# Joining the left-over rows of a feed-forward width of 2752, and the time-step columns of a state-space layer, into full tiles

## The reference

```python
D_FF = 2752                          # 21 * 128 + 64
def conv_ffn(h, w_up, conv_w, conv_b, w_down):
    u = h @ w_up                     # 1024 -> 2 * 2752
    up = jnp.pad(u, ((0, 0), (CONV_WIDTH - 1, 0), (0, 0)))
    c = conv_b + conv_w[0] * up[:, 0:S]
    for tap in range(1, CONV_WIDTH): # CONV_WIDTH = 3
        c = c + conv_w[tap] * up[:, tap:tap + S]
    gate, val = jnp.split(c, 2, axis=-1)
    return (jax.nn.silu(gate) * val) @ w_down
...
# first layer of the second block: of h @ w_in_a, 16 columns are the time steps of 16 heads
dt = jax.nn.softplus(dt_raw.astype(f32) + dt_bias.astype(f32))
```

## Time and profile before

| | |
|---|---|
| time, median of 3 runs | 1671.64 us (1670.78 to 1671.84) |
| span of the profiled execution, first to last instruction | 1668.0 us |
| PE busy | 96% of the span, 8762 matmuls |
| PEld, DVE, ACT, POOL busy | 81%, 62%, 50%, 6% |
| DMA, mean over the span | 81 GB/s |
| mean granted clock of TensorE | 0.986 |

### The profile page before, as it was taken

One profiled execution on the slowest core, in us unless ns is written; L12 is line 12 of the kernel. 1 busy time (PEld: TensorE's weight loads), 2 busy tenths in 40 slices (PEclk: granted clock), 3 DMA queues, 4 the chain that ended last, 5 costly groups with the idle time before them and its releaser, 6 DMA issues.

```text
span 1668.0 us, 23619 instructions
## 1 busy us (share of the span) xinstructions
PE 1597.5 (96%) x8762; PEld 1357.1 (81%) x8762; DVE 1027.0 (62%) x1784; ACT 833.5 (50%) x1598; POOL 94.2 (6%) x159
## 2 busy tenths in 40 slices
PE   7998899999999999999999999999999998999988
PEld 6987787887788888887788889788877787888877
DVE  5567986886555656555234434797666556548873
ACT  6645566665434555553123213786453563336763
POOL 1321400001000000000000000000000000000000
PEclk9999999999999999999999999999999999999999
DMA  7531012122543333332222232111122212131011
GB/s 214 149 92 43 31 58 70 45 70 83 169 136 83 92 94 86 96 88 93 93 90 81 92 101 87 47 51 53 53 76 85 68 51 76 59 112 54 26 51 51
DMA packets 148960, 135.61 MB, mean 81 GB/s; under 512 B 9072, under 2 KB 142960, under 8 KB 148864
## 3 DMA queue, kind: packets, MB, share of 16 engines
q1 hardware_dynamic: 143744, 120.04, 23.6%
q0 software_dynamic: 4544, 13.67, 2.5%
q10 hardware_dynamic: 576, 0.60, 0.1%
HBM read 124.07 MB, written 7.34 MB: 79 GB/s over the span
## 4 chain that ended last, share of the span: by engine, by line
PE 76%; DVE 13%; ACT 6%; issue 4%; DMA 1%; POOL 0%; DVEq 0%; SPq 0%; ACTq 0%
PE bank L299 21%; PE bank L301 20%; PE bank L300 20%; PE bank L1239 2%; PE bank L1253 1%; PE bank L1216 1%; ACT whi L277 1%; DVE wlo L284 1%; DVE pr L1404 1%; DVE ptl L1409 1%; PE bank L2783 1%; PE bank L2083 1%; ACT pr L3200 1%; DVE nm L1392 1%; ACT pr L1297 1%
## 5 line engine op out<-in xcount | busy, mean ns | idle before, releaser
L299 PE MATMUL bank<-hh,whi 128*128 128x512 f32 (+3 forms) x1208 | 466.1, 386 | 17.3 <-DVE wlo L284 6.3
L301 PE MATMUL bank<-hh,wlo 128*128 128x512 f32 (+3 forms) x1208 | 455.7, 377 | 0.0
L300 PE MATMUL bank<-hl,whi 128*128 128x512 f32 (+3 forms) x1208 | 455.0, 377 | 0.0
L277 ACT ACTIVATE whi<-wraw 128x2048 fp32r<-128x2048 f32 x111 | 212.6, 1915 | 285.4 <-PE bank L301 285.3
L284 DVE TENSOR_TENSOR wlo<-wraw,whi 128x2048 fp32r<-128x2048 f32 x101 | 231.3, 2290 | 157.0 <-ACT whi L277 156.2
L299 PEld LDWEIGHTS bank<-hh,whi 128*128 128x128 f32 (+2 forms) x1208 | 229.9, 190 | 60.7 <-issue 6.0
L301 PEld LDWEIGHTS bank<-hh,wlo 128*128 128x128 f32 (+2 forms) x1208 | 229.6, 190 | 43.5
L300 PEld LDWEIGHTS bank<-hl,whi 128*128 128x128 f32 (+2 forms) x1208 | 230.4, 191 | 38.8 <-issue 0.2
L299 PE MATMUL bank<-ah,whi 128*128 128x512 f32 (+1 forms) x240 | 87.6, 365 | 3.9 <-DVE al L3323 2.5
L1409 DVE TENSOR_TENSOR ptl<-bank,pth 128x128 fp32r<-128x128 f32 (+3 forms) x128 | 56.7, 485 | 52.4 <-ACT pth L1315 52.0
L1297 ACT ACTIVATE pr<-bank,nm 128x128 f32<-128x128 f32 (+3 forms) x128 | 66.8, 533 | 42.5 <-DVE nm L1392 42.5
(11 more groups left out here) (417 smaller groups left out, 3081.7 us busy)
## 6 DMA issues: line engine op xcount, KB each, us to landing
wraw<-in_w_in_a_dram SPq DMA_DIRECT2D x52, 512.0 KB, 4.5
wraw<-in_w_up_dram SPq DMA_DIRECT2D x42, 512.0 KB, 4.8
wraw<-in_w_in_dram SPq DMA_DIRECT2D x34, 512.0 KB, 4.8
wraw<-in_w_in_c_dram SPq DMA_DIRECT2D x18, 512.0 KB, 4.8
wraw<-in_w_down_dram SPq DMA_DIRECT2D x16, 512.0 KB, 4.0
wraw<-in_w_out_a_dram SPq DMA_DIRECT2D x16, 512.0 KB, 4.0
aside<-stage POOLq DMA_DIRECT2D x20, 256.0 KB, 2.3
wraw<-in_w_attn_br_dram SPq DMA_DIRECT2D x8, 512.0 KB, 4.3
```

The lines of the kernel that those rows point to most:

```text
L277: act.activation(whi[:, p], wraw[:, p], ACT.Copy).then_inc(w_hi_done, 1)
L299: pe.matmul(out, ws[0], hs[0], start=first, stop=False)
L300: pe.matmul(out, ws[0], hs[1], start=False, stop=False)
L301: return pe.matmul(out, ws[1], hs[0], start=False, stop=last)
```

## The change

1. **Up.** The last up item is loaded with its 64 value columns right behind its 64 gate columns, and is one tile of 24 matmuls on 128 columns: gate in rows 0 to 63 of the bank, value in rows 64 to 127. The parameters of the value columns are put on rows 64 to 127 too. ACT and DVE treat the two row halves by as many instructions as before, 64 rows each; the Silu reads rows 0 to 63 and writes rows 64 to 127. The high part of the 64 products goes to rows 64 to 127 of the last slot of `yh`, the low part to rows 0 to 63 of the same slot (`low_beside`).
2. **Down.** The last 64 rows of `w_down` are loaded twice, to rows 0 to 63 and 64 to 127 (a DMA of 128 rows of 1 KB, before 64). Two matmuls on 128 rows (`beside`: high and low part of the weight by that slot of `yh`) stand where three on 64 rows stood.
3. **Time steps.** DVE writes the low part of the 16 columns into `whi` itself, 32 columns behind the high part, and no longer makes the whole `wlo` of that item. The tile is 16 matmuls on 48 columns into bank 4, and DVE adds the two row groups: `daf` takes two chained operations, before one. The wait for `drained` ahead of this tile is gone, and the next stage waits for `drained` to be two less, so no longer for the time-step tile.

```diff
         def pairs(b, c0, cols):
             s = wraw[:, b % 2]
-            return [(s[:, :, 0:cols], v[:, :, bass.ds(c0, cols)]), (s[:, :, P:P + cols], v[:, :, bass.ds(c0 + DFF, cols)])]
+            return [(s[:, :, 0:cols], v[:, :, bass.ds(c0, cols)]),
+                    (s[:, :, cols:2 * cols], v[:, :, bass.ds(c0 + DFF, cols)])]
...
+        def low_beside(dve):
+            dve.wait_ge(f_high, FT + 1)
+            dve.tensor_tensor(yh[GATE, FT, :], fa[VALUE, LJ, :], yh[VALUE, FT, :].bitcast(F32),
+                              ALU.subtract).then_inc(f_low, 1)
...
+        LAST, LJ = n0 + FT, FT % 2
+        GATE, VALUE = slice(0, FREST), slice(P - FREST, P)
         @block.tensor
         def _(pe):
             halved_items(pe, n0, ready, between)
-            each(1, pe, lambda b, j, i, f, n: products(pe, b, j, i, f, n))
+            each(1, pe, lambda b, j, i, f: products(pe, b, j, i, f))
+            item_ready(pe, LAST)
+            pe.wait_ge(drained, m0 - 4 + 2 * FT + 1)
+            tile_of(pe, LAST, 0, bank[2 * LJ][:, :], H).then_inc(tiles, 2)
...
+            straight(act, LAST, LJ, 0, FT)
+            split_hi(act, LAST + 2)
+            gate(act, LJ, FT, GATE, VALUE)
+            high(act, LJ, FT, VALUE)
...
+            conv(dve, LAST, LJ, 0, FT)
+            product(dve, LJ, FT, VALUE)
+            split_lo(dve, LAST + 2)
+            low_beside(dve)
...
                             pr_ = [(s[:, 0:FT - 16, :], v[:, 16:FT, cols]),
-                                   (s[0:FREST, FT - 16, :], mat[FT * P:DFF, cols])]
+                                   (s[:, FT - 16, :], mat[FT * P:DFF, cols].unsqueeze(0).to_broadcast([2, FREST, IC]))]
...
+            def beside(pe, p, t, out, ts):
+                cs = slice(P * t, P * t + P)
+                pe.matmul(out[:, ts], whi[:, p, FT - 16, cs], yh[:, FT, ts], start=False, stop=False)
+                return pe.matmul(out[:, ts], wlo[:, p, FT - 16, cs], yh[:, FT, ts], start=False, stop=True)
...
-                        k, cs = FT - 16, slice(P * t, P * t + P)
-                        mm = passes(pe, out, (whi[0:FREST, p, k, cs], wlo[0:FREST, p, k, cs]),
-                                    (yh[0:FREST, FT, :], yl[0:FREST, FT, :]), False, True)
+                        mm = beside(pe, p, t, out, slice(0, S))
...
             item_ready(pe, n0 + 6)
-            pe.wait_ge(drained, m0 + 9)
-            tile_of(pe, n0 + 6, 0, bank[0][0:SSD_H, :], H, cols=SSD_H).then_inc(tiles, 2)
+            for k in range(KT):
+                for part in H:
+                    mm = pe.matmul(bank[4][0:LO + SSD_H, :], whi[:, (n0 + 6) % 2, k, 0:LO + SSD_H], part[:, k, :],
+                                   start=(k == 0 and part is hh), stop=(k == KT - 1 and part is hl))
+            mm.then_inc(tiles, 2)
...
-            split_lo(dve, n0 + 6)
+            dve.wait_ge(w_hi_done, n0 + 7)
+            dt = (n0 + 6) % 2
+            dve.tensor_tensor(whi[:, dt, :, LO:LO + SSD_H], wraw[:, dt, :, 0:SSD_H],
+                              whi[:, dt, :, 0:SSD_H].bitcast(F32), ALU.subtract).then_inc(w_lo_done, 1)
...
-            dve.tensor_scalar(daf[0:SSD_H, :], bank[0][0:SSD_H, :], pcol("dt_bias", rows=SSD_H), None,
-                              ALU.add).then_inc(drained, 1)
+            dch(dve, dve.tensor_scalar(daf[0:SSD_H, :], bank[4][0:SSD_H, :], pcol("dt_bias", rows=SSD_H), None,
+                                       ALU.add))
+            dve.tensor_tensor(daf[0:SSD_H, :], bank[4][LO:LO + SSD_H, :], daf[0:SSD_H, :], ALU.add).then_inc(drained, 1)
...
-            pe.wait_ge(drained, m0)
+            pe.wait_ge(drained, m0 - 2)
             tile(0)
```

More of the change, by code:

```diff
@@ L89, in tiles, with value_tiles @@
         return out.reshape(n, P).T
+    def value_tiles(v):
+        out = tiles(v)
+        out[P - FREST:, FT] = out[:FREST, FT].copy()
+        return out
     def rows(v):
@@ L107, in pack_params @@
         "convw_g": np.concatenate([tiles(cw[t, :DFF]) for t in range(3)], axis=1),
-        "convw_v": np.concatenate([tiles(cw[t, DFF:]) for t in range(3)], axis=1),
-        "convb_g": tiles(cb[:DFF]), "convb_v": tiles(cb[DFF:]),
+        "convw_v": np.concatenate([value_tiles(cw[t, DFF:]) for t in range(3)], axis=1),
+        "convb_g": tiles(cb[:DFF]), "convb_v": value_tiles(cb[DFF:]),
         "norm_a": tiles(a["norm_a_2"]),
@@ L1668, in two_blocks @@
     yh = at("yh", Y, [FT + 1, S], F32R)
-    yl = at("yl", Y + 44 * K, [FT + 1, S], F32R)
+    yl = at("yl", Y + 44 * K, [FT, S], F32R)
     cg = at("cg", SC_AT, [2, S])
@@ L1693, in _, with products @@
                 load_item(sp, n0 + f, 0, pairs(n0 + f, P * f, P if f < FT else FREST))
-        def products(pe, b, j, i, f, cols):
+        def products(pe, b, j, i, f):
             item_ready(pe, b, i)
@@ L1699, in products, with halves_of, rows_at, straight @@
                 pe.wait_ge(drained, m0 - 4 + 2 * f + t + 1)
-                tile_of(pe, b, t, bank[2 * j + t][0:cols, :], H, cols=cols).then_inc(tiles, 1)
-        def straight(act, b, j, i, f, n):
-            for t, (wn, bn, dst) in enumerate((("convw_g", "convb_g", cg), ("convw_v", "convb_v", cv))):
+                tile_of(pe, b, t, bank[2 * j + t][:, :], H).then_inc(tiles, 1)
+        def halves_of(j, f):
+            both = (("convw_g", "convb_g", cg), ("convw_v", "convb_v", cv))
+            if isinstance(f, int) and f == FT:
+                return [(w_, b_, d_, bank[2 * j], r) for (w_, b_, d_), r in zip(both, (GATE, VALUE))]
+            return [(w_, b_, d_, bank[2 * j + t], slice(0, P)) for t, (w_, b_, d_) in enumerate(both)]
+        def rows_at(name, col, rows):
+            return parm[rows, bass.ds(PCOL[name] + col, 1)]
+        def straight(act, b, j, i, f):
+            for t, (wn, bn, dst, src, rows) in enumerate(halves_of(j, f)):
                 act.wait_ge(tiles, 2 * b + 4 * i + t + 1)
@@ L1724, in conv, with gate, product @@
                 dve.sem_inc(drained, 1)
-        def gate(act, j, f, n):
+        def gate(act, j, f, rows=slice(0, P), to=slice(0, P)):
             act.wait_ge(f_conv, 4 * f + 2)
-            act.activation(cg[0:n, j, :], cg[0:n, j, :], ACT.Silu).then_inc(f_silu, 1)
-        def product(dve, j, f, n):
+            act.activation(cg[to, j, :], cg[rows, j, :], ACT.Silu).then_inc(f_silu, 1)
+        def product(dve, j, f, rows=slice(0, P)):
             dve.wait_ge(f_silu, f + 1)
@@ L1748, in each @@
                 for j in range(2):
-                    body(n0 + j, j, i, 2 * i + j, P)
-            for f in rest:
-                body(n0 + f, f % 2, 0, f, P if f < FT else FREST)
+                    body(n0 + j, j, i, 2 * i + j)
+            if FT % 2:
+                body(n0 + FT - 1, (FT - 1) % 2, 0, FT - 1)
+        LAST, LJ = n0 + FT, FT % 2
+        GATE, VALUE = slice(0, FREST), slice(P - FREST, P)
         @block.tensor
@@ L1827, in halved @@
                 half_tile(pe, b, t, out, (yh, yl), h, kts=FT - 16, k0=16, first=False, last=False)
-                k, cs, ts = FT - 16, slice(P * t, P * t + P), token_half(h)
-                return passes(pe, out[:, ts], (whi[0:FREST, b % 2, k, cs], wlo[0:FREST, b % 2, k, cs]),
-                              (yh[0:FREST, FT, ts], yl[0:FREST, FT, ts]), False, True)
+                return beside(pe, b % 2, t, out, token_half(h))
             for c in range(2):
```

45 lines of the change are left out of this document (22 added, 23 removed).

## The result

| | before | after |
|---|---|---|
| median of 6 runs | 1671.21 us (1669.22 to 1673.95) | 1656.96 us (1656.08 to 1662.36) |
| ratio to before | | 0.9925, 95% interval 0.9906 to 0.9944 |
| profiled execution: time / span / granted clock | 1670 us (below) / 1668.0 / 0.986 | 1660.67 us / 1658.7 us / 0.983 |

The change makes the kernel faster by 0.75%, 12.5 us (9.4 to 15.7 by the interval); the two medians alone lie 14.3 us apart. I had forecast 1661.0, with a range from 1658.9 to 1664.8.

The account below looks back on a forecast made before the run. PE was taken to bound the kernel, with three quarters of the span. Terms 4.63 + 3.96 + 1.00 + 1.02 = 10.6 us, taken from 1671.6, gave 1661.0 us, range 1658.9 to 1664.8.

Parts of the forecast that it names:

- part 1, up: End of up: PE loses one 24-matmul tile; down starts 4.74 us earlier, less 0.11 for a slow first step: 4.63 us.
- part 2, six slots and half 0: Last down slots: 0.66 us saved six times (3.96), plus 0.50 twice on 256 tokens, first token half (1.00).
- the change of shape: Last down slots: entering and leaving 64 rows costs 0.43 us on 512 tokens, 0.38 on 256.
- part 2, half 1: Last down group, second token half: its 1.0 us saved becomes idle PE, as DVE's `wlo` sets the next stage: 0.
- part 3 with the clock up: Time steps: next stage starts 1.25 us earlier, less 0.23 at its third tile: 1.02 us, bounds 0.3 to 1.25.
- the level: Whole time: median of runs stays 3.6 us above the profiled span, so 1671.6 - 10.6 = 1661.0 us.
- The clock falls: Longer idle PE at time steps or after down brings 3 us half clock, costing 1.5: 1662.5 or 1664.0; chance 17%.
- The 64-row slots cost the same: Last down slots: delay due to something that stays, not shape; down gives 1.6 instead of 4.96: 1664.4; chance 10%.
- The down loads come late: Third down items: doubled 128-row loads land late, making the kernel slower; 1675 at 14.6 us landing; chance 3%.
- The reverse: A half-clock stretch is not met any more because all work moves: 1659.5 us; chance 7%.

Follow-up runs that it names:

- up alone: Changed kernel with the time steps as before and the joined up tile's products brought back to rows 0 to 63, three 64-row passes in down: 1667.77 us, 0.9986.
- down alone: Kernel before, with only the low part written beside the high one, the load broadcast and two matmuls per last down slot: 1665.71 us, ratio 0.9976.
- time steps alone: Kernel before, with only the time-step change added (16 matmuls, low part in `whi`): 1670.41 us, ratio 1.0000.
- after the third time: The changed kernel, unchanged, executed and profiled once more: 1657.73 us, ratio to before 0.9925.
- Feed-forward alone: Changed kernel with the time steps put back as before, so only the up and down changes: 1658.93 us (0.9928), then 1657.50 us (0.9924).
- three passes on 128 rows: Kernel before, with the last down slot multiplied on 128 rows, zeros in the lower rows and all three passes kept: 1666.95 us, ratio 0.9976.
- after again: The changed kernel, unchanged, executed a second time: 1657.66 us, ratio to before 0.9923.
- the reordered kernel: Changed kernel with the next stage's split before the last taps, and the first `xt` addition and two ACT preparations moved earlier: 1659.40 us, ratio to before 0.9931.

## Why the prediction missed

**The terms held.** By the local lengths:

| step | forecast | measured |
|---|---|---|
| part 1, up: 4.74, less the slow first step 0.11 | 4.63 | 4.76 - 0.14 = 4.62 (up alone) |
| part 2, six slots and half 0 | 3.96 + 1.00 | 4.92 (down alone) |
| of it the change of shape | 3.3 | 3.32 |
| part 2, half 1 | 0 | 0 |
| part 3 with the clock up | 1.02 | 0.97 (time steps alone, and after the third time) |
| part 3 where the clock fell | | 22.47 - 22.83 = -0.36 |

So the sum, 10.6 by forecast, is 9.51 + 0.97 = 10.5 by rows, and 9.51 - 0.36 = 9.15 where the clock fell at the time steps. From the end of up to down I had 0.8 us, and it is 774.03 - 773.19 = 0.84.

**The step that failed is the level.** "The median of the runs is 3.6 above that span, and I take the same distance." In all 153 executions of this study whose span is on record, the time lies 1.74 to 2.18 us above the span, 2.0 on average. The 3.6 was not a distance between a time and its span. It was one between the median of three runs, which lies 1.2 us above the mean of the 73 later ones (below), and the span of an execution that was a little faster than that mean: by the distance of 2.0 the profiled one took about 1668.0 + 2.0 = 1670.0 us, not 1671.6. I had compared a single span with a median and called the difference fixed. With 2.0 the forecast would have been 1659.4, nearer, and the range would have begun at 1657.3 and still missed.

**The spread of executions was left out of the range.** The same program took 1666 to 1677 us (before, 73 executions, mean 1670.45, standard error 0.26) and after 1653 to 1665 (18, mean 1658.26, standard error 0.7). Most of that goes with the mean granted clock of the execution: a straight line through all of them, with one level for each kernel, gives 1.29 us for 0.001 of the clock (standard error 0.07), and leaves a scatter of 1.2 us about it. A range of 6 us made of terms alone had no room for six executions whose median could lie 1 or 2 us from the mean. By steps, from 1661.0 to 1656.96:

- the distance, 3.6 to 2.0: -1.6, so 1659.4;
- the execution profiled before was itself 0.45 below the mean of its kernel (1670.0 against 1670.45): +0.45, so 1659.85;
- the 18 executions of after had a mean clock higher by 0.00117 than those of before (0.98483 against 0.98366): -1.5, so 1658.35, which is the mean of after, 1658.26, within its error;
- the six executions of the result have a median 1.3 below that mean.

At equal clock (by that line), after is 10.68 ± 0.66 us faster than before, where the rows say 10.5 and the forecast 10.6; each ± here is a 95% interval, about twice the standard error. The 12.2 that the means show (I had 10 to 12 for it) is that and the clock. Feed-forward alone stands at 9.67 ± 0.78 (rows 9.51), three passes on 128 rows at 3.39 ± 0.86 (rows 3.32), time steps alone at 0.44 ± 0.76 (rows 0.97). These agree with the rows. Down alone, at 3.94 ± 0.78 (rows 4.92), and up alone, at 2.8 ± 0.8 (rows 4.62), don't: they fall short by 2.4 and by 4.8 standard errors.

**The rivals.** *The clock falls* was right as a mechanism, at one of the two places that I named. Behind the 1.95 us of idle PE at the time steps it fell in 2 of 4 profiles (after, and after again; not after the third time, nor time steps alone), and cost 1.33 us each time, near the 1.5 that I had. With 1.37 us of idle (the kernels without part 3) it stayed up in all profiles. Behind down it fell in every profile within 7 us of the start of the next stage, whether PE had been idle for 1.65 us or for 2.45, so the change added no fall there: the 24 us from that start have a clock of 0.86 in all 13 profiles. *The 64-row slots cost the same*: refuted by the run on 128 rows. *The down loads come late*: refuted by the rows of ACT and by down alone. *The reverse*, stretches of half clock that are met no more, is open (next).

**What stays open.** Whether the higher clock of the kernels with both feed-forward parts is a property of them or chance, and with it whether some 1.5 us of the 12.2 belong to the change. The 30 executions of after and of feed-forward alone have a mean clock near 0.985, and the 85 of before and of time steps alone 0.9836. The difference of 0.0013 is 3.3 times its standard error, which is much for chance; but up alone (0.9830) and down alone (0.98355) don't show it, nor does the reordered kernel (0.9838, 5 executions).

Nor do the pieces add up in whole times, at equal clock 2.8 ± 0.8 for up and 3.9 ± 0.8 for down against 9.7 ± 0.8 for both, while their local lengths add up to 0.03 us. The two profiles show a place outside A to E that takes part of the gain back. From the first matmul of the stage behind down to the first time-step matmul, up alone took 333.0 us and down alone 332.8, where eight other profiles took 331.4 to 331.6 and three 329.8 to 329.9. It arises at once, as the first 24 us of that stage in up alone show:

```profile
901.38:925.38 24.00, 21.68 (x146) 20.81 (x147) 14.74 (x32) 7.78 (x16) 0.00 (x0) 0.86 0.29 89
```

That is 146 matmuls (148 in down alone) where all the other 11 profiles have 159, at the same mean clock of 0.86: 11 to 13 matmuls on 256 tokens, 1.3 to 1.6 us at 0.12 each. The half clock is as long, but lies elsewhere. In these two the granted clock is 1.00 for the first 5.5 us of the stage, and the half clock comes behind them in one stretch; in the other 11 the clock is 0.50 from 1.5 to 3.5 us already, and there are two stretches. So the mean clock alone doesn't tell what half clock costs, and "at equal clock" is no finer than that. Whether the other executions of these two kernels are like their profiles isn't on record.

## What to carry to other kernels

Where an engine runs without gaps, start times at two ends of a stretch with the count of steps between give prices that hold to 0.1 us, for a removed matmul as for a change of shape; and a stage's first instruction gains only up to what is late next, which must be looked up each time. A small piece of matmul on fewer rows pays for its way in and out beside its work (0.43 us beside 0.68 for three matmuls on 512 tokens, 0.38 beside 0.36 on 256), so put it on all rows, if only with zeros. A forecast of the whole time needs two things beside the terms: the time of the profiled execution itself (here its span and 2.0 us), and the scatter of executions (here 2.2 to 3.0 us, one standard deviation), which is larger than the terms for half 0 and for the time steps.

## What the hardware showed that I had not expected

**Half-clock stretches wander.** The same window at the head of the up stage, where the three programs are the same so far, in the kernel before, in after and in feed-forward alone:

```profile
530.00:540.00 10.00, 8.10 (x58) 6.93 (x58) 7.43 (x17) 4.38 (x8) 0.00 (x0) 1.00 0.40 107
```

```profile
530.00:540.00 10.00, 8.70 (x42) 8.14 (x42) 4.94 (x10) 3.08 (x5) 0.00 (x0) 0.66 0.47 131
```

```profile
530.00:540.00 10.00, 8.27 (x49) 7.29 (x49) 6.62 (x14) 3.86 (x7) 0.00 (x0) 0.83 0.40 109
```

With the clock at 1.00 PE does 58 matmuls in the 10 us, at 0.66 it does 42. Each profile has 41 to 58 us of half clock in 9 to 12 stretches, besides a last one at its very end in which PE has nothing left to do, and between two profiles of one program some of them come and go. The 1.29 us for 0.001 of the mean clock fits that (0.001 of 1660 us is 1.66 us, less what falls where PE waits anyway), and it is why a gain of 1 us could be seen in a window and not in a time.

**A change of shape costs by rows, not by columns.** The way into a slot on 64 rows and out of it again loses 0.43 us together on 512 tokens and 0.38 on 256; from 128*128 to 128*64 and back, and into 128*48 or 128*16, the step stays at 0.23 (the way out of the last two lies ahead of an idle stretch and can't be read). The Trainium skill's rule ("TensorEngine Tiling (Array Packing)", Key Properties) that changing the tiling mode drains TensorE is borne out here for rows alone.
